# Attention outputs with features on the partitions, probabilities scaled on ScalarE, one more step in three attentions

## The reference

```
mixer_a: 16 query heads of 64, 4 key heads, window of 128, a sink logit per head
mixer_b: 3 groups of q, k, v with 16 heads of 64 each, dilations 1, 4, 16;
         o = sum_g softmax(lse)_g * o_g     (one softmax over the keys of the three groups)
mixer_c: 16 heads of 64, causal within a block of 256 (here the whole sequence)

s = q @ k.T * dh**-0.5;  s = where(ok, s, NEG);  m = s.max(-1)
p = exp(s - m);  l = p.sum(-1)  (+ exp(sink - m) in A)
o = (p @ v) / l
out = o.reshape(S, 1024) @ w_o
```

## Time and profile before

| | us |
|---|---|
| median of 3 runs (lowest, highest) | 2409.44 (2409.36, 2410.32) |
| span of the profiled execution, first to last instruction | 2408.6 |
| PE busy in it | 2375.2 (99%) |
| DVE busy | 1633.0 (68%) |
| ACT busy | 1122.9 (47%) |
| POOL busy | 184.1 (8%) |

### The profile page before, as it was taken

How to read it: one execution, slowest core, us unless ns; L and a number is a source line. 1 busy time by engine, 2 the same in 40 slices (tenths; PEclk the granted TensorE clock), 3 DMA queues, 4 the chain that set the end, 5 groups by cost and what they waited for, 6 DMA issues and landing times.

```text
span 2408.6 us, 33578 instructions
## 1 busy us (share of the span) xinstructions
PE 2375.2 (99%) x13648; PEld 2001.8 (83%) x13648; DVE 1633.0 (68%) x2282; ACT 1122.9 (47%) x1570; POOL 184.1 (8%) x190
## 2 busy tenths in 40 slices
PE   7999999999999999999999999999999999999999
PEld 5788888787888878887888888888888888988887
DVE  7866755557667576668776777677676577687664
ACT  4544344444443434435443455564444365574442
POOL 1210002021000320001100100000000000001000
PEclk9999999999999999999999999999999999999999
DMA  6465343335553446543755344444755344445652
GB/s 247 142 202 209 140 175 140 141 140 171 197 209 140 163 165 215 191 158 128 262 188 179 136 175 157 155 179 149 279 180 188 113 167 156 173 175 181 225 177 91
DMA packets 259080, 419.09 MB, mean 174 GB/s; under 512 B 11984, under 2 KB 149200, under 8 KB 258928
## 3 DMA queue, kind: packets, MB, share of 16 engines
q1 hardware_dynamic: 254064, 400.15, 46.7%
q0 software_dynamic: 4864, 16.80, 2.1%
HBM read 415.86 MB, written 1.05 MB: 173 GB/s over the span
## 4 chain that ended last, share of the span: by engine, by line
PE 92%; DVE 4%; ACT 2%; DMA 1%; issue 1%; POOL 0%; SPq 0%; DVEq 0%; ACTq 0%
PE bank_L L2431 21%; PE bank_L L2447 17%; PE bank_S L2811 8%; PE bank_T L2776 7%; PE bank_L L2776 7%; PE bank_O L2811 7%; PE bank_L L2428 4%; PE bank_T L2781 4%; PE bank_L L2781 4%; PE bank_O L2724 1%; DVE wlo L1631 1%; PE bank_S L2431 1%; PE bank_O L2431 1%; PE bank_T L2398 1%; PE bank_T L2707 1%; PE bank_T L2386 1%
## 5 line engine op out<-in xcount | busy, mean ns | idle before, releaser
L1631 DVE TENSOR_TENSOR wlo<-raw,whi 128x2048 fp32r<-128x2048 f32 x316 | 718.0, 2290 | 123.4 <-ACT whi L1237 123.0
L1237 ACT ACTIVATE whi<-raw 128x2048 fp32r<-128x2048 f32 x290 | 542.5, 1894 | 55.3 <-DMA raw<-in_w_out 13.2
L2431 PE MATMUL bank_L<-whi,xt 128*128 128x512 f32 (+2 forms) x1632 | 495.8, 386 | 3.3 <-ACT tok L1283 2.1
L2447 PE MATMUL bank_L<-whi,xt 128*128 128x512 f32 x1248 | 389.2, 393 | 3.3 <-DVE xt L1645 2.1
L2431 PEld LDWEIGHTS bank_L<-whi,xt 128*128 128x128 f32 x1632 | 295.9, 188 | 61.2 <-ACT tok L1283 3.3
L2431 PE MATMUL bank_L<-wlo,xt 128*128 128x512 f32 (+2 forms) x816 | 311.4, 382 | 0.0
L2447 PEld LDWEIGHTS bank_L<-whi,xt 128*128 128x128 f32 x1248 | 230.6, 188 | 51.9 <-DVE arena L1737 2.9
L1503 ACT ACTIVATE tok<-tok 128x256 f32<-128x256 f32 x96 | 40.1, 417 | 449.5 <-DVE tok L2137 449.5
L2447 PE MATMUL bank_L<-wlo,xt 128*128 128x512 f32 x624 | 243.6, 390 | 0.0
L2776 PE MATMUL bank_T<-xt,whi 128*128 128x512 f32 x768 | 192.3, 392 | 0.0
L2776 PE MATMUL bank_L<-xt,whi 128*128 128x512 f32 x768 | 191.7, 392 | 0.0
(11 more groups left out here) (353 smaller groups left out, 3630.3 us busy)
## 6 DMA issues: line engine op xcount, KB each, us to landing
raw<-in_w_gate_up SPq DMA_DIRECT2D x176, 512.0 KB, 5.9
raw<-in_w_in SPq DMA_DIRECT2D x72, 1024.0 KB, 6.8
draw<-in_w_down SPq DMA_DIRECT2D x44, 1024.0 KB, 6.2
raw<-in_ffn_w_up SPq DMA_DIRECT2D x88, 512.0 KB, 5.8
raw<-in_b_w_qkv SPq DMA_DIRECT2D x36, 1024.0 KB, 6.9
draw<-in_ffn_w_down SPq DMA_DIRECT2D x22, 1024.0 KB, 6.2
raw<-in_w_lift SPq DMA_DIRECT2D x16, 1024.0 KB, 6.2
raw<-in_a_w_qkv SPq DMA_DIRECT2D x12, 1024.0 KB, 8.2
```

What stands on the lines that cost most here:

```text
L1237: act.activation(wide(whi, w, nkc, ncols)[:, ks, :], wide(raw, w, nkc, ncols)[:, ks, :], ACT.Copy) \
L1631: dve.tensor_tensor(wide(wlo, w, nkc, ncols)[:, ks, :], wide(raw, w, nkc, ncols)[:, ks, :], wide(whi, w, nkc, ncols)[:, ks, :].bitcast(F32 ...
L2431: mm = pe.matmul(banks[name][:, 0:st["ncols"]], xx[:, kk, t * P:(t + 1) * P], ww[:, kk, :], start=(kk == 0 and q == 0), stop=(kk == nkc - ...
L2447: mm = pe.matmul(banks[bank][:, :], xx[:, k, t * P:(t + 1) * P], ww[:, k, :], start=(k == 0 and q == 0), stop=(k == KC - 1 and q == 2))
```

## The change

Kinds A and DSA get a stage `spread` in place of `attention` (memory attention keeps the old one). Kinds B and C keep `paired`. In all of them:

- PE's product with v has v (128 keys by 64 features) as the stationary factor and the transposed probabilities as the moving one, 128 or 256 queries wide. The two heads of a pair go to the two column halves of the array, so that their 128 features land on the partitions of bank_O, in 128 or 256 columns. A bank of 512 columns collects 4 heads, and is held until DVE has read it.
- ACT multiplies the probabilities in SBUF in place by the reciprocal (`scales`, `pair_scales`), before PE transposes them; the transposes wait for a new semaphore `scaled`. DVE's reciprocal is one step earlier in `paired`.
- A group of 4 heads is evacuated by one `group_high` (ACT) and one `group_low` (DVE) of 512 columns, straight into the two parts. Neither r nor `yb` is written, `halves` and the turns are gone.
- In A the transposes stand at step i-3 (was i-2) and the products of two heads come together at steps 5, 7, and so on, so the loop has 20 steps where it had 19. In DSA the transposes stay at i-2.
- The first groups of B and C are written to yt_hi/yt_lo, and a class `Joined` gives the projection both buffers. The rope's scratch is r in place of hg_values.

The core of the diff, in the order: the stages of A and DSA, ACT in `paired`, ACT in `spread`, DVE in `paired`, PE in `spread`, PE in `paired`:

```
+            for i, u in enumerate(units):
+                edge, ps = 1 if u["sink"] else 0, stride * (i % ring)
...
-                attention(units, [(turn_done, n["turn"]), (dev, n["dev"])], first, behind, in_twos=True, turned=hv)
+                spread(units, [(turn_done, n["turn"]), (dev, n["dev"])], first, behind, to, 3, 5, 400,
+                       lows={18: (n["w"] + 1, (0,))})
...
+            spread(units, [(aev, small_ok[1])], (turn_done, n["turn"]), [], to, 2, 4, 384, fill=fill,
+                   highs={4: (a_w + 1, (0,)), 6: (a_w + 1, (1,))},
...
-                    def pair_evacuate(j):
+                    def pair_scales(j):
                         act.wait_ge(rl_done, U0 + j + 1)
-                        act.wait_ge(pv_done, U0 + j + 1)
...
+                                ins = act.activation(smflat[:, q], smflat[:, q], ACT.Copy, scale=rl2[:, c:c + 1])
+                            ins.then_inc(scaled, 1)
+                    def group_high(g):
+                        to = st["to"]
+                        act.wait_ge(pv_done, V0 + (g + 1) * to["per"])
+                        act.activation(to["dst"][g][0], banks[st["ob"][g % 2]][:, :].rearrange("p (k s) -> p k s", s=SEQ),
+                                       ACT.Copy).then_inc(thi_done, 1)
...
-                        if i >= 2:
-                            pair_evacuate(i - 2)
+                        if i < len(J):
+                            pair_scales(i)
+                        if i >= 2 and (i - 1) % st["to"]["per"] == 0:
+                            group_high((i - 2) // st["to"]["per"])
...
+                        if i < len(U):
+                            exps(i)
+                        if 1 <= i <= len(U):
+                            scales(i - 1)
+                        if i > lag and (i - lag) % 4 == 0:
+                            group_high((i - lag) // 4 - 1)
...
                             pair_copies(i - 1)
-                            pair_reciprocal(i - 1)
+                        if i < len(J):
+                            pair_reciprocal(i)
+                        if i >= 2 and (i - 1) % st["to"]["per"] == 0:
+                            group_low((i - 2) // st["to"]["per"])
                         if i in st["ropes"]:
                             rotated(st["ropes"][i])
...
-                        for g, _ in st["groups"].get(i, ()):
-                            group_lo(st["rows"], g)
...
+                    def values_of_two(i):
+                        g, q = divmod(i // 2, 2)
+                        name = OB[g % 2]
+                        if q == 0:
+                            take(name)
+                        pe.wait_ge(pt_done, at["pt"] + i + 2)
+                        for s, (c0, c1) in enumerate(((0, 2 * P), (2 * P, 3 * P))):
+                            for w in range(2):
+                                u = U[i + w]
+                                mm = pe.matmul(banks[name][w * HD:(w + 1) * HD, q * SEQ + s * P:(q + 1) * SEQ], u["rows"][1][1][s],
+                                               pflat[:, u["pts"] + c0:u["pts"] + c1], start=(s == 0), stop=(s == 1))
...
+                        if 0 <= i - lag < len(U):
+                            turned(i - lag)
+                        if i > lag and (i - lag) % 2 == 0:
+                            values_of_two(i - lag - 2)
...
-                            pe.wait_ge(p_done, u["p0"] + 1)
+                            pe.wait_ge(scaled, u["sc0"] + 1)
...
-                        for g, _ in st["groups"].get(i, ()):
-                            turn_group(st["rows"], g)
```

More of the change, by code:

```diff
@@ L450, in pool_splits, with across, paired @@
             add("pool_splits", ws=ws, after=after)
-        def halves(src):
-            st = add("halves", src=src, dst=(xt_hi, xt_lo), at_tp=[None] * 4, when=[None] * 4)
-            n["sg"] += 4
-            return st
-        def paired(pairs, first, qb, ob, ps_at, pts_at, fill=(), turns=(), ropes=(), splits=(), groups=(), parts=(), turned=None):
-            at_turns, at_groups = dict(turns), dict(groups)
+        def across(dst, per, place):
+            st = dict(dst=dst, per=per, place=place, sg=n["sg"])
+            n["sg"] += len(dst)
+            return st
+        def paired(pairs, first, qb, ob, ps_at, pts_at, to, fill=(), turns=(), ropes=(), splits=(), parts=()):
+            at_turns = dict(turns)
             st = add("paired", pairs=pairs, first=first, qb=qb, ob=ob, fill=[q for q, _, _ in fill], turns=at_turns,
-                     ropes=dict(ropes), splits=splits, groups=at_groups, parts=parts, rows=turned, out=None)
+                     ropes=dict(ropes), splits=splits, parts=parts, to=to, out=None)
             for late, a, b in fill:
@@ L472, in paired @@
                     u["pieces"], off, bank, used = [], edge, 0, 0
-                    for row, (pieces, _, _) in enumerate(u["rows"]):
+                    for row, (pieces, _) in enumerate(u["rows"]):
                         for mask, products in pieces:
@@ L742, in build @@
                 part(late[0], 0, 3)
-                hv = halves(r)
+                both = across([[q[:, 2 * g:2 * g + 2, :] for q in (((yt_hi, yt_lo), (xt_hi, xt_lo))[g // 2])] for g in range(4)],
+                              2, lambda q: q * SEQ)
+                to = [both, dict(sg=both["sg"] + 2)]
                 pairs = []
@@ L1413, in _, with exps, scales, group_high @@
                             pair_copies(i - 1)
-                        if i >= 2:
-                            pair_evacuate(i - 2)
+                        if i < len(J):
+                            pair_scales(i)
+                        if i >= 2 and (i - 1) % st["to"]["per"] == 0:
+                            group_high((i - 2) // st["to"]["per"])
                         if i in st["turns"]:
                             heads_hi(st["turns"][i])
-                        for g, _ in st["groups"].get(i, ()):
-                            group_hi(st["rows"], g)
+                elif st["kind"] == "spread":
+                    U, to, lag = st["units"], st["to"], st["lag"]
+                    def exps(i):
+                        u, k = U[i], at["unit"] + i
+                        act.wait_ge(ttr_done, at["ttr"] + T * (i + 1))
+                        for row, q in enumerate(u["exp"]):
+                            ins = act.activation(smflat[:, q], smflat[:, q], ACT.Exp, bias=nb[:, k % 4, row:row + 1], scale=-1.0,
+                                                 accum_out=ls[:, k % 4, row:row + 1])
+                        ins.then_inc(p_done, 1)
+                    def scales(i):
+                        u, k = U[i], at["unit"] + i
+                        act.wait_ge(rl_done, k + 1)
+                        for row, (c0, c1) in enumerate(((0, P), (P, 3 * P))):
+                            q = slice(u["ps"] + c0, u["ps"] + c1)
+                            ins = act.activation(smflat[:, q], smflat[:, q], ACT.Copy, scale=rl[:, k % 4, row:row + 1])
+                        ins.then_inc(scaled, 1)
+                    def group_high(g):
+                        act.wait_ge(pv_done, at["pv"] + 2 * (g + 1))
+                        act.activation(to["dst"][g][0], banks[OB[g % 2]][:, :].rearrange("p (k s) -> p k s", s=SEQ),
+                                       ACT.Copy).then_inc(thi_done, 1)
+                    for late in st["fill"]:
+                        after(late)
+                    for i in range(st["steps"]):
+                        if i < len(U):
[4 more added lines that the diff above has]
+                            group_high((i - lag) // 4 - 1)
+                        if i in st["highs"]:
+                            split_hi(*st["highs"][i])
+                        for late, t in ends(st["fill"], i - 1, st["steps"]):
+                            evacuated(late, t, LB[t])
+                    for late, t in ends(st["fill"], st["steps"] - 1, st["steps"]):
+                        evacuated(late, t, LB[t])
@@ L2502, in _ @@
                     if st["begun"]:
-                        turn_group(st["begun"]["rows"], 3)
                         output(st, 1, 1, 0, 4)
```

292 lines of the change are left out of this document (183 added, 109 removed).

## The result

The changed kernel takes 2451.24 us (median of 4 runs, 2445.29 to 2452.66) against 2409.4: 1.0172 times as long, interval 1.0158 to 1.0187. The forecast was 2423.7 with a range of 2405 to 2431. The direction was right, the size was not: +41.8 us where +14.3 had been worked out. The profiled execution has a span of 2449.1 us, and the granted clock is 0.991 on average, where it was 1.000.

A forecast was written before the change was run, and what follows sets the result against it. PE was taken as the bound (92% of the chain), with ACT near its limit in A. A +6.4, B +6.3, C +2.6 and DSA -1.0 gave +14.3 on 2409.4, so 2423.7 us, range 2405 to 2431.

The forecast's parts named there:

- What is removed and the product's price: Turns of finished rows on PE go, worth at most 12.5 us; A's product of two heads costs 0.86 us, 0.14 less.
- The rival of colliding column halves: Products of two heads run one after the other on PE: 33 us more, about 2456; chance 0.07 together with the clock.
- ACT's price and A's bound: In A, scales cost ACT 0.69 us a head, 1.69 in all against PE's 1.35, so A becomes bound by ACT.
- A's sum: Two sliding-window attentions: projection starts at 85.95, as if at 82.8 before, so each loses 3.2 us, +6.4 together.
- 15 x (0.88 + 0.69), three group evacuations: ACT's time in A's loop: exps and scales of 15 heads, 23.55 us, plus three evacuations of 0.49, 1.47.
- B: Attention in two halves beside projections: later evacuations and rope cost +6.3 us, within half to one and a half times that.
- +0.75 after three turns ... are gone: B's second half: PV(4) waits for group_low(0) and copies come late, net +0.75 us after three turns are removed.
- -0.45: The turn inside B's projection is removed, which takes 0.45 us off.
- C: Attention with two heads a step: at step 3 the rope starts later and PE waits, +2.6 us (2.1 to 3.0).
- "0" for the copies and transposes behind group_low and the scales: Later in C: four removed turns, 1.9 us with 0.5 idle, are cancelled by later copies and transposes, net 0.
- DSA: Two attentions: turns and PV save 0.9 and 0.56 us, a wait for scales adds 0.95; -0.5 each, -1.0 together.
- The clock: Rival: in A, PE busy some 80% falls to 1.2 GHz, costing more than all other terms; chance 2 in 100.

The follow-up runs named there:

- e2: The change with only the order moved: scales behind evacuations and rope ahead in B and C, group_low behind copies in A and DSA; 2423.23 us.
- e6: e2 with one more 128-column activation on ACT for each head of A, writing to memory nobody reads; 2429.14 us, median of three.
- e7: e2 with e8's edits in B and C, and GpSimd scaling the 256 columns of each head of A; 2405.94 us.
- e5: The change with one thing moved: in A and DSA group_low stands behind the copies of the step; 2438.86 us.
- e9: e1 with 20, 24 and 30 identity transposes that nobody reads in PE's three longest waits; 2421.89 us.
- e1: The change with kind A put back to its form of before, B, C and DSA kept as changed; 2430.79 us.
- e4: The change with 312 more transposes on PE, of the identity and read by nobody, ahead of its waits; 2443.47 us.
- e8: e3 with the last group_low of B's first half behind two ropes, and parts of the output projection ahead of products; 2404.18 us.
- e10: e7 with 10 identity transposes that nobody reads ahead of the first head's transposes in A; 2404.58 us.
- e3: The change with kind A as before (e1's edit) and e2's order in B and C; 2412.17 us.

## Why the prediction was wrong, point by point

- **What is removed and the product's price.** Right. No L2491 group is left in A, B, C, 0.80 us for the product of two heads against 0.86 taken. The rival of colliding column halves is refuted by that row.
- **ACT's price and A's bound.** Right in mechanism and size, and shown: scales 0.69 us, projection at 86.38 in e2 against 85.95, +3.2 us. ACT is busy without a gap in e2 and a head takes 1.57 us; e6 (more load on ACT, slower) and e7 (less, faster) agree.
- **A's sum.** Wrong as a forecast of the change itself: +10.5 and +9.4. The step that failed is "15 x (0.88 + 0.69), three group evacuations": it took ACT to run back to back. DVE's order (group_low, waiting for group_high, ahead of the copies) makes PE wait 1.1 to 1.2 us, which then delays scores, maxima and exps, so that ACT is idle (22.34 busy of 25). By the distances of heads that is 1.5 us in the loop of each A. The rest above +3.2 was not parted into waits and clock; the two A hold 12.0 of the 22.1 us of shortfall. e5 moves this one call and gains 12.4 us, waits and clock together.
- **B.** +15.2 against +6.3. The first half, 4.5 forecast, is +5.9, and +4.3 where the clock stays full (e9): the rope behind group_low (2.5 forecast; the wait grew from 0.32 to 2.75) and the later evacuations (0.9 to 1.45 forecast; the waits grew from 0.69 to 1.73 and 1.93, and from 0.47 to 2.0) were right. The second half, 1.75 forecast, is +9.3, and +3.8 in e9. Two steps failed there. One is "+0.75 after three turns ... are gone": group_low(0) behind scales and group_high gave a wait of 3.43, and a stretch at half the clock behind it. The other is that the projection was credited with its turn alone ("-0.45"), while the wait for the layer norm behind it grew by 1.1 (0.89 to 2.00).
- **C.** +5.8 against +2.6. The rope's wait was 3.34 instead of 1.01, 2.3 more where 2.6 was forecast; the clock was at half from 874.0 to 877.5 behind it, a shortfall of 1.7. The other 1.8 are not traced to an instruction; in the sum they stand against the "0" for the copies and transposes behind group_low and the scales. The forecast carried over the rope's time of before, in which the last instruction took 1.12 us beside a cast of GpSimd; in the change it took 0.28, which was luck: e1, e4, e5 and e9 have 1.12 again.
- **DSA.** Right. The wait of 0.95 is there, and the gain is -0.7 each against -0.5.
- **The clock.** This is, by the estimate below, the largest term that was missing. It was named as a rival at 2 in 100, with a fall in A only; the sum gave it nothing and priced each wait at its length. In the change it fell to half in A, in B, behind B and in C, with a shortfall of 22.1 us in all. Behind waits in B and C 4.6 of 5.1 us of shortfall were paid (e9), in A's loop 1.8 of 3.4 (e2); at these two rates the 22.1 cost some 12 to 20 of the 41.8 us, an estimate. How the 41.8 divide exactly between waits and clock is not settled, since a wait and the slow stretch behind it come and go together: moving calls (e2) took 28.0 us away and 15.3 of the shortfall with them. With e4's transposes the clock is at 0.999 and the kernel still 36 us slower than before, part of it by those transposes.

Of the 27.5 us that the sum missed, then, some 12 to 20 come from pricing a wait at its length, and the rest are waits and loads that the sum had too small or left out.

## What to carry to other kernels

A long wait of PE can cost more than its length, since a stretch at half the clock may follow it; read the granted clock in short windows, and where a forecast adds waits of several us, price that stretch too: at nearly its whole shortfall where PE works without a gap, at less where another engine is the limit. A call that waits for another engine belongs behind everything in its queue that others wait for (here copies, ropes and evacuations ahead of group_low and scales); 28 of 42 us came back by order alone (e2). Where a step would be moved to an engine that is busy for over 90% of a stage (ACT in A, 22.84 of 25 us), leave that stage out (e8), or split the step with an idle engine (e7, e10).

## What the runs showed of the hardware that was not expected

- The clock fell behind PE's waits, but not by their length alone. Past the first 40 us, every wait of 3.3 us or more (3.34, 4.88 and 4.93 in the change, e5 and e1, and 3.43 in each of them) had a stretch at half the clock behind it. The wait of 2.76 at the end of the first half of B had one in e1 and e2 (2.75 in the change and e5), none in e3 (2.76) and e6 (2.75). The wait of 2.0 behind B had one in four kernels and none in seven, and behind a wait of 1.51 in A the clock fell in the second A of e2 and not in the first. With idle transposes in three waits of e1 there was none (e9). From 450 on, e1 and then e3:

```profile
450.00:455.00 5.00, 2.65 (x12) 2.30 (x13) 3.39 (x13) 2.19 (x4) 0.00 (x0) 0.82 1.02 394
455.00:460.00 5.00, 5.00 (x20) 4.07 (x19) 4.01 (x2) 2.76 (x2) 0.00 (x0) 0.84 0.04 13
```

```profile
450.00:455.00 5.00, 3.93 (x22) 3.40 (x23) 2.69 (x12) 3.24 (x4) 0.00 (x0) 1.00 0.82 317
```

- At half the clock 512 columns take 0.43 us instead of 0.23.
- GpSimd multiplies 128x256 in place by a column of scalars in 0.93 us while ACT and DVE work on the same tiles, and DVE's copies of 384 columns beside it take 0.54 us as in e2. Its casts of 1024 columns take 1.04 us in the median and 1.45 on average (52 in the change), since some take 3.1.
- Beside such a cast DVE's rope instructions of 128x128 take 1.0 to 1.1 us instead of 0.28 (e1 and the change, step 3 of C).
